# A fused pooling and sliding-window attention layer in float32: input norm applied at the outputs, and a first stage worked in three token groups

## What is computed

```python
xn = h * rsqrt(mean(h*h) + EPS) * norm_g              # per token: a factor of the token times norm_g
u, zp, q, k, v, za, ga, gb = split(xn @ w_in)         # widths 1024,1024,1024,256,256,1024,1024,1024
ya = multiscale_pool(u, state) * silu(zp)
q, k = rope(rms_norm(q)), rope(rms_norm(k))           # 16 query heads, 4 key heads, of 64
yb = windowed_attention_with_sinks(q, k, v, caches) * silu(za)
m  = sigmoid(ga) * (ya @ w_proj_pool) + sigmoid(gb) * (yb @ w_proj_attn)
h  = h + m @ w_out
h  = h + sigmoid(h @ w_ple_gate) * (p @ w_ple)
```

## Time and profile before

| what | us |
|---|---|
| runs | 1221.38, 1218.24, 1220.37 (median 1220.37) |
| the profiled execution, its own time | 1219.35 |
| its span in the trace | 1217.4 |
| PE busy | 1185.9 |
| DVE busy | 556.7 |
| ACT busy | 399.7 |
| POOL busy | 413.3 |

### The profile page before, as it was taken

The page is one execution under the profiler, slowest core; times in us unless marked ns, Lnnn a source line. Parts: engine busy times, 40 slices in busy tenths (PEclk is TensorE's granted clock), DMA queues, the critical chain, the costliest instruction groups (busy, mean ns, idle before and its releaser), DMA issues.

```text
span 1217.4 us, 19199 instructions
## 1 busy us (share of the span) xinstructions
PE 1185.9 (97%) x7514; PEld 1162.2 (95%) x7514; DVE 556.7 (46%) x947; ACT 399.7 (33%) x882; POOL 413.3 (34%) x189
## 2 busy tenths in 40 slices
PE   5899999999999999999999999999999999999998
PEld 4899999999999999999999999999999999999998
DVE  5857776100466666665552444650142251164322
ACT  3343434323466665656420110141131030031112
POOL 2334444322222211222333344513244335254420
PEclk8899999999999999999999999999999999999999
DMA  7414646522343334434061111144232233232211
GB/s 278 137 36 104 183 120 179 168 56 67 93 115 116 99 97 126 120 113 123 36 223 38 48 34 48 34 146 160 93 100 89 74 130 112 71 105 64 77 37 54
DMA packets 113611, 124.88 MB, mean 103 GB/s; under 512 B 14175, under 2 KB 101239, under 8 KB 113551
## 3 DMA queue, kind: packets, MB, share of 16 engines
q1 hardware_dynamic: 98359, 100.04, 26.2%
q10 hardware_dynamic: 15192, 24.00, 6.9%
HBM read 88.93 MB, written 37.12 MB: 104 GB/s over the span
## 4 chain that ended last, share of the span: by engine, by line
PE 79%; DVE 13%; ACT 5%; issue 2%; DMA 0%; DVEq 0%; SPq 0%; ACTq 0%
PE ps L577 69%; ACT prob L1478 4%; PE ps L756 3%; DVE prob L1100 2%; DVE sa L1040 2%; DVE v_low L1118 1%; DVE ps L1120 1%; PE ps L892 1%; DVE xn L975 1%; DVE sa L1036 1%; DVE m_lo L979 1%; DVE sa L1125 1%; PE ps L604 1%; PE ps L746 1%; PE ps L772 1%
## 5 line engine op out<-in xcount | busy, mean ns | idle before, releaser
L577 PE MATMUL ps<-m_hi,w_hi 128*128 128x352 f32 x1992 | 654.9, 330 | 7.5 <-DVE m_lo L979 7.5
L577 PE MATMUL ps<-m_lo,w_hi 128*128 128x352 f32 x1992 | 641.7, 323 | 0.0
L577 PE MATMUL ps<-m_hi,w_lo 128*128 128x352 f32 x1992 | 430.2, 324 | 0.0
L577 PEld LDWEIGHTS ps<-m_hi,w_hi 128*128 128x128 f32 x1992 | 375.9, 189 | 11.2 <-issue 5.0
L577 PEld LDWEIGHTS ps<-m_lo,w_hi 128*128 128x128 f32 x1992 | 375.5, 189 | 1.3
L577 PEld LDWEIGHTS ps<-m_hi,w_lo 128*128 128x128 f32 x1992 | 340.8, 188 | 0.0
L512 POOL TENSOR_TENSOR w_hi<-raw_a,w_one 128x1024 fp32r<-128x1024 f32 x42 | 82.3, 1958 | 741.8 <-PE ps L577 511.4
L514 POOL TENSOR_TENSOR w_lo<-raw_a,w_hi 128x1024 fp32r<-128x1024 f32 x42 | 111.7, 2658 | 3.3
L514 POOL TENSOR_TENSOR w_lo<-raw_b,w_hi 128x1024 fp32r<-128x1024 f32 x42 | 109.0, 2595 | 3.3
L512 POOL TENSOR_TENSOR w_hi<-raw_b,w_one 128x1024 fp32r<-128x1024 f32 x42 | 92.7, 2208 | 0.0
L1464 ACT ACTIVATE pt_hi<-ps 128x512 fp32r<-128x512 f32 x64 | 38.2, 599 | 103.0 <-PE ps L756 103.0
(11 more groups left out here) (205 smaller groups left out, 1161.6 us busy)
## 6 DMA issues: line engine op xcount, KB each, us to landing
raw_a<-in_w_in SPq DMA_DIRECT2D x26, 512.0 KB, 3.7
raw_b<-in_w_in SPq DMA_DIRECT2D x26, 512.0 KB, 3.8
qk_d<-qkst ACTq DMA_DIRECT2D x20, 512.0 KB, 5.8
gate_d<-gst ACTq DMA_DIRECT2D x16, 528.0 KB, 3.0
gin<-gate_d SPq DMA_DIRECT2D x16, 528.0 KB, 3.7
qt<-qk_d SPq DMA_DIRECT2D x32, 256.0 KB, 3.1
xT_d<-sa SPq DMA_DIRECT2D x4, 1056.0 KB, 7.4
yb_d<-sa SPq DMA_DIRECT2D x1, 4224.0 KB, 12.8
```

The costliest lines, as they stand in the source:

```text
L577: last = nc.tensor.matmul(ps[:, 3 * parity + c, 0:CH], w, x[:, k, CH * c:CH * c + CH], start=(k == 0 and w is wh and x is src_hi), stop=(k ...
```

## The change

The token factor is no longer applied to the input. `m_hi` and `m_lo` now hold the input times `norm_g` alone, and every consumer of a tile applies the factor: `rbc` on the tiles of `za`, `ga`, `gb`, `u` and `zp`, the per-row factors `rs` on the v rows, and for q and k only the EPS of their norm is adapted (`ems`). The emptying of those tiles with `rbc` is DVE's now, and was ACT's.

The opening works in three token groups (384, 384 and 288 tokens) by 8 feature blocks, 24 units. For each unit PE transposes, ACT rounds straight from PSUM, DVE takes the low part from PSUM and copies the raw block to `sa`, and PE does 6 matmuls. Six units are transposed ahead, later ones two ahead. The first half of the first weights is loaded ahead of `x_prompt`. `xT_d` is stored in three pieces, the last after unit 23. The factors reach `rbc` later, by three rounds in tile 2.

The third turn back moves from step 6 to step 7 in even tiles. Several buffers share memory (`v_low` and `pst` lie in `kv_out`, `gtmp` and `sg` in `rbc`). The diff, cut to its core:

```diff
# SP
+            load_half(0)
+            for t in range(3):
+                load_x(t)
+            load_half(1)
+            for t in range(3, PBLK):
+                load_x(t)
...
+            load_chunk(1, w_in, COL["q"])
+            for g, (c0, w) in enumerate(GROUPS):
+                sp.wait_ge(x_raw, KT * (g + 1))
+                sp.dma_start(xT_d[:, :, c0:c0 + w].rearrange("k p n -> p k n"), sa[:, :, c0:c0 + w])\
+                    .then_inc(xt_stored, 16)
# PE: the units
+UNIT_BANK = [1, 2, 4, 5, 6, 7, 1, 2] + [5, 6, 7, 2] * 2 + [6, 7] * 4
...
+            for t in range(3):
                 pe.wait_ge(x_loaded[t], 16)
+                for i in range(6):
+                    turn_unit(i, t)
+            for i in range(len(UNITS)):
+                if i + 2 >= 6 and i + 2 < len(UNITS):
...
+                    pe.wait_ge(x_raw, UNIT_PRIOR[nxt] + 1)
+                    for t in tiles:
+                        turn_unit(nxt, t)
+                unit_products(i)
# unit_products(i), for both tiles h
+                pe.wait_ge(x_hi, i + 1)
+                for h in range(2):
+                    product(h, w_hi, m_hi, start=(k == 0))
+                    product(h, w_lo, m_hi)
+                pe.wait_ge(x_split, i + 1)
+                for h in range(2):
+                    last = product(h, w_hi, m_lo)
# DVE: the units, and the factors
+            for i, (g, k) in enumerate(UNITS):
+                c0, w = GROUPS[g]
+                dve.wait_ge(x_hi, i + 1)
+                v.scalar_tensor_tensor(m_lo[:, k, c0:c0 + w], ps[:, UNIT_BANK[i], 0:w], g8[:, k:k + 1],
+                                       m_hi32[:, k, c0:c0 + w], ALU.mult, ALU.subtract).then_inc(x_split, 1)
+                v.tensor_copy(sa[:, k, c0:c0 + w], ps[:, UNIT_BANK[i], 0:w]).then_inc(x_raw, 1)
...
+            dve.wait_ge(xt_stored, 16 * len(GROUPS))
+            v.tensor_copy(rms_rows[PBLK], rs[0:NS, 3, PBLK:PBLK + 1].to_broadcast([NS, P]))
+            v.tensor_copy(sa[:, 6, 0:SEQ].rearrange("p (t n) -> p t n", n=P),
+                          rs[:, 3, 0:PBLK].unsqueeze(2).to_broadcast([P, PBLK, P])).then_inc(rms_done, 1)
# DVE: v tiles, before keep_kv and split_rows
                     dve.wait_ge(rows_free, 3 * j + 3)
+                    blocks = rows[:, j % 3, :].rearrange("p (t n) -> p t n", n=P)
+                    step.did(v.tensor_tensor(blocks, blocks, rs[:, 3, :].unsqueeze(2).to_broadcast([P, PBLK + 1, P]),
+                                             ALU.mult))
+                    step.settle()
                     keep_kv(j)
                     split_rows(j)
# DVE: za tiles (one after the sample scores are read, one at the end of each turn of the loop)
+                v.tensor_tensor(thirds(out), pset(h), thirds(rbc[:]), ALU.mult).then_inc(set_free[h], 1)
...
-            tile_free(dve, GATE_TILE + 6)
-            tile_free(dve, GATE_TILE + 7)
+            dve.wait_ge(za_done, KT)
# DVE: ga and gb tiles, last in attention_half
                     gate_output(u - 1, (m - 1) % 8, bass.ds(i * (2 * P) + ((m - 1) // 4) * P, P))
+                if m % 2:
+                    h = m // 2
+                    scale_gate(i * 4 + h, h % 2, None if first and h < 2 else i * 2 + h // 2)
+
+            def scale_gate(m, h, stored):
+
+                dve.wait_ge(tile_done, m + (GATE_TILE + KT + 1))
+                if stored is not None:
+                    dve.wait_ge(gate_stored[h], stored * 16)
+                v.tensor_tensor(thirds(gst[:, h, :]), pset(h), thirds(rbc[:]), ALU.mult).then_inc(set_free[h], 1)
# DVE: pooling groups; three tensor_tensor with rbc fill ub, then after r_ready of both tiles:
+                for h in range(2):
+                    dve.wait_ge(tile_done, POOL_TILE + 6 * g + 2 + h + 1)
+                    v.tensor_tensor(thirds(zs[:, h, :]), pset(h), thirds(rbc[:]), ALU.mult).then_inc(set_free[h], 1)
                 if g == 3:
                     for kk in range(6):
+                        split_lo(kk, kk + 1)
                 for h in range(2):
                     n = POOL_TILE + 6 * g + 4 + h
                     dve.wait_ge(tile_done, n + 1)
-                    tile_free(dve, n - 2)
+                    dve.wait_ge(zp_done, k + 1)
# ACT: pooling groups
-                    act.wait_ge(tile_done, g * 6 + (POOL_TILE + 2 + h + 1))
-                    a.activation(thirds(zs[:, h, :]), pset(h), ACT.Silu).then_inc(set_free[h], 1)
+                    act.wait_ge(set_free[h], g * 3 + (POOL_TILE // 2 + 2))
+                    a.activation(zs[:, h, :], zs[:, h, :], ACT.Silu).then_inc(zp_done, 1)
                     take_history(k, k + 1)
# ACT: gates
-                a.activation(thirds(gst[:, h, :]), pset(h), ACT.Copy).then_inc(set_free[h], 1)
                 act.wait_ge(set_free[h], gate_half[0] + (GATE_TILE + KT) // 2 + 1)
                 act.dma_start(gate_d[m], gst[:, h, :]).then_inc(gate_stored[h], 16)
# plan_rounds
+            for i in range(3):
+                here.append(((3, 4, 4)[i], "rms", 0, i, r))
...
-            rows(1, (3, 5, 5))
+            rows(1, (5, 6, 6))
...
-                back(j - 3, (3, 5, 6))
+                back(j - 3, (3, 5, 6 if j % 2 else 7))
```

More of the change, by code:

```diff
@@ L617, in turn @@
                     emptied, n = FREED[r - 2]
-                    pe.wait_ge(rows_free if emptied == "rows" else back_free, n)
+                    pe.wait_ge({"rows": rows_free, "back": back_free, "rms": rms_free}[emptied], n)
                 bank = 6 + r % 2
-                if kind == "rows":
-                    src = sa[:, 7 * (j % 2), :]
+                if kind == "rms":
+                    pe.wait_ge(rms_done, 1)
+                    for b in range(4 if i < 2 else 0):
+                        last = nc.tensor.transpose(ps[:, bank, P * b:P * b + P], rms_rows[4 * i + b], ident)
+                    if i == 2:
+                        last = nc.tensor.transpose(ps[:, bank, 0:NS], rms_rows[PBLK], ident[0:NS, 0:NS])
+                elif kind == "rows":
+                    src = sa[:, 7 * (j % 2), :] if j >= 2 else first[:, j, :]
                     if i == 0:
@@ L660, in rounds @@
                 for step, kind, jj, i, r in plan:
-                    if kind not in ("rows", "back"):
+                    if kind not in ("rows", "back", "rms"):
                         continue
@@ L961, in _ @@
[L961 to L980 removed]
+            v.memset(rs[:, 0, :], 1.0).then_inc(ssq_init, 1)
@@ L1336, in _ @@
                     .then_inc(ssq_done, 1)
[L1337 to L1344 removed]
+            act.wait_ge(par_loaded, 16)
@@ new lines, in _ @@
+            for i, (g, k) in enumerate(UNITS):
+                c0, n = GROUPS[g]
+                act.wait_ge(x_turned, i + 1)
+                a.activation(m_hi[:, k, c0:c0 + n], ps[:, UNIT_BANK[i], 0:n], ACT.Copy, scale=g8[:, k:k + 1])\
+                    .then_inc(x_hi, 1)
+                if i in SQUARE_OF:
+                    square_x(SQUARE_OF[i])
+                if i in (13, 21):
+                    b = i // 8 - 1
+                    act.wait_ge(group_done, b + 1)
+                    for j in range(2):
+                        a.activation(first[:, j, GROUPS[b][0]:GROUPS[b][0] + 3 * P], ps[:, 3 * j + b, 0:3 * P], ACT.Copy)
@@ new lines, in _ @@
+            for j in range(2):
+                act.wait_ge(tile_done, j + 1)
+                a.activation(first[:, j, 6 * P:T], ps[:, 3 * j + 2, 0:T - 6 * P], ACT.Copy).then_inc(set_free[j], 1)
+            act.wait_ge(ms_done, 1)
+            a.activation(rs[:, 2, :], rs[:, 1, :], ACT.Sqrt).then_inc(std_done, 1)
+            act.wait_ge(hist_done, 1)
+            a.activation(hist[:].rearrange("p (a k) n -> p a (k n)", a=2), ps[:, 6:8, 0:4 * nh], ACT.Copy)\
+                .then_inc(hist_copied, 1)
@@ L1501, in attention_tiles @@
                         gate_half[0] = i * 2 + h // 2
-                        gate(i * 4 + h, h % 2, None if first and h < 2 else i * 2 + h // 2)
+                        gate(i * 4 + h, h % 2)
             sink_column(0)
```

266 lines of the change are left out of this document (118 added, 148 removed).

## The result

The changed kernel takes 1233.06 us (median of 4 runs, 1230.97 to 1234.28), beside 1220.88 for the kernel before on the same chip (1218.24 to 1222.97): ratio 1.0099, 95% interval 1.0073 to 1.0125. The forecast was 1232.0. The medians are 12.2 apart. The profiled execution's span is 1232.5 us against 1217.4 before, 15.1 more: at 1234.28 it is the slowest of the four, with a mean granted clock of 0.994 where the other three have 0.996.

What follows compares the result with a forecast made beforehand. PE bounds the kernel (busy 97%), in attention a ring of waits through ACT and DVE. Terms -17.8 + 1.0 - 2.8 + 5.0 + 2.0 + 18.0 + 7.3 = +12.7 on 1219.35 gave 1232.0 us, range 1223 to 1240.

Steps and rivals of the forecast that it cites:

- The opening: Start of the kernel up to tile 2: its products begin at 44.6 us, 17.8 earlier, with bounds 40 and 49.
- the slow start: First products of the opening: 1.5 us charged for a low clock after sparse transposes, between 0 and 6.
- The turns: PE's 54 transposes of the opening's later units: at most 8.6 us, taken as 6.5.
- The 1.0 for waits on banks: Opening's last group: only two PSUM banks serve the transposes, which wait for DVE's copy behind ACT's squares, 1.0 us.
- Rounds, step 7 and v rows: Tiles 2 to 11: factor rounds +1.0, turns back at step 7 -2.8, DVE's v-row multiply delaying PE +5.0 us.
- Entry of attention: Before attention's first masks: DVE's scale of the last `za` tile delays PE's first turn, +2.0 us (0 to 3).
- the slack of 0.6: Entry of attention: spare 0.6 us before a later end of DVE's clearing delays PE's first turn of probabilities.
- The ring: Attention loop, PE to ACT to DVE to PE: DVE's gate-tile scale adds 1.2 us in 15 places, +18.0.
- The rival in which the ring absorbs the scales: Attention loop: gate-tile scales cost 0 instead of 1.2 us per place, giving 1214 us; chance 0.08.
- Pooling: Pooling stage: waits of 0.9 and 2.4 us for history turns and 4.0 before the projection, +7.3 (3 to 9).
- Behind pooling: All stages after pooling: predicted to move by 0 us.
- a rival at 0.12: Clock stays low for much of the opening or drops in new 4 to 5 us idle stretches: +6, 1238; chance 0.12.

Runs made afterwards that it cites:

- run 2: Changed kernel with each attention gate tile scaled one unit later, where VectorE idles before its reciprocals; 1217.71 us, ratio 0.9982 to the kernel before.
- run 4: Changed kernel with each later opening unit transposed right before its own products, none ahead, instead of two ahead; 1251.69 us, ratio 1.0257 to the kernel before.
- run 6: Changed kernel with VectorE's six low parts made before, not after, the second gate-tile scale of the last pooling group; 1227.55 us, ratio 1.0062 to the kernel before.
- run 7: Changed kernel with ScalarE's history copies in pooling taken before its SiLU waits for the gate scale; 1229.35 us, ratio 1.0071 to the kernel before.
- run 3: Changed kernel with VectorE's raw copies in the opening cut to 8 columns per unit (wrong residual); 1232.79 us.
- run 10: The kernel of run 9 with the sample loop's second gate tile scaled before the wait for the sample's output; 1202.96 us, ratio 0.9857 to the kernel before.
- run 1: Changed kernel with 14 of the 16 gate-tile scales in attention cut from 1056 columns to 32; 1219.21 us, ratio 0.9993 to the kernel before.
- run 9: Changed kernel with the four reorderings of run 2, run 6, run 7 and run 8 together; 1204.93 us, ratio 0.9873 to the kernel before.
- run 5: Changed kernel with each later opening unit transposed one unit ahead instead of two; 1233.83 us.
- run 8: Changed kernel with the last query tile's low parts taken before the value rows are split; 1227.96 us, ratio 1.0065 to the kernel before.

## Why the prediction was right, step by step

- **The opening** (-17.8): -17.5. The sum held, and its terms missed both ways. The first products came 0.7 later than put, and the slow start that I charged with 1.5 cost 0.85 (the first six products took 1.90 instead of 1.05). The turns were charged with 6.5, under a bound of 8.6 that should have read 8.9 (54 times 0.66/4); they took some 8 (32.1 us from 12.06 to 44.15, less 23.1 of products and the 0.85), 0.33 a unit at first and 0.6 in the last group. The 1.0 for waits on banks did not come. Part of the gain is the clock, too, which I had not counted: the first products of the kernel before ran at 0.50 from 33.05 to 37.3, some 2.1 lost. In the changed kernel the clock column says 1.00 at the slow start all the same. The Trainium skill (TensorE: Matmul & The Clock Gate, section Part 4: PE-mode transpose) holds that transposes do not count for the clock. The slow first unit behind 18 transposes agrees. The rise in the earlier trace rows speaks against it, and so do runs 2, 4, 6 and 7, in whose profiles the products behind the same transposes start without a slow spacing. Either way it was under 1 us. That DVE's copies do not bound it: run 3. That it needs the turning ahead: run 4.
- **Rounds, step 7 and v rows** (+3.2): +4.6. The wait of 3.0 did go. The `v` wait was 3.6 and not 5.0, because the multiply kept its short length and the split had been slow already; but the low clock behind it cost another 2.6, which no term of mine held. Two misses, of which one hides half of the other.
- **Entry of attention** (+2.0): +1.2, from PE's first gate product to its first turn (10.70 before, 11.94 after); the slack of 0.6 held, and the delay before it was mis-sized. The last clearing ended 1.9 later, not 2.6 (4.1 after the first gate product before, 5.9 after), because the multiplication ahead of it took 0.79 instead of 1.64. Run 10 recovers all of the 1.2.
- **The ring** (+18.0): +16.0 (17.27 less 1.24). Place and mechanism held (runs 1 and 2). The term was mis-sized per place: 1.06, not 1.2, since a clearing and a short gap before the masks lie beside the scale (run 1). The rival in which the ring absorbs the scales is refuted by run 1, though run 2 shows how near it lay: the same work one unit later is absorbed whole.
- **Pooling** (+7.3): +8.0. The waits are 1.1, 2.2 and 4.0, against 0.9, 2.4 and 4.0 forecast; for the other 0.7 no wait shows.
- **Behind pooling** (0): +2.8. This is the step that failed: I gave the clock in new idle stretches to a rival at 0.12 instead of putting it in the sum. It happened at both long waits, at 2.6 and 3.0 (the first is in the stage from tile 2 to the end of `za`), and in every other profile with such waits, at 1.4 to 3.1. The errors in the ring and at the entry (-2.7 together) hid it in the total.

So the total was right by the mechanism in its four main terms (opening, ring, v rows, pooling), and by luck in its last 2 to 3 us. Part of that is which execution one holds it against: the forecast of 12.7 more lies close to the 12.2 between the medians, and 2.4 short of the 15.1 between the two profiled executions, whose changed one lost more to the clock than its three fellows.

## What to carry to other kernels

An instruction moved onto an engine that idles half the time can still cost nearly its full length (1.06 of 1.26 us here): look in the chain of waits for the idle stretches inside the loop, and put it there, not where its input happens to be ready. A new wait of 3.6 to 4.0 us on TensorE in the middle of dense work cost its own length and 1.4 to 3.1 us more in this kernel, as the granted clock was 0.50 behind it every time; it belongs in the sum with both parts. When work moves from one engine to another, write down anew what that engine's queue holds behind it; the five losses here (ring, end of pooling, history, `v` rows, entry) went by order alone, with no work taken out. Two orders that are each good can meet, though: the low parts and the history copies together leave PE a new wait of 2.2 (run 9).

## What the runs showed that I had not expected

- All 16 waits of 3.6 or 4.0 us in the profiles of the changed kernel and runs 1 to 8 went with a clock of 0.50, for some 3 to 6 us of full work. The 2.2 us wait for the history copy in the last pooling group did it in three executions of eight (runs 2, 4 and 6), the 2.2 us wait at the mixing tile in one of two (run 10). The 15 waits of 1.2 in the ring never did.
- The clock can fall without one long wait: in run 4, from 45.2 on, behind a stretch with waits of at most 0.8 in which PE was busy for 7.3 of 10 us. From 14 to 44 us the clock had stayed at 1.00 under much the same pattern (PE busy for 22.4 of 30).
- At the start of the program the clock column shows 1.00 while products run at about half pace (0.32 apart instead of 0.18); there the spacing of the matmuls has to be read instead.
